# Third layer's attention: the exponential's bias and the reciprocals made for two tiles at once on VectorE

## The reference, cut to what matters

```python
# third layer, h = head, q: 256 latent rows, k: 512 rows (context and latent)
s = einsum('qd,kd->qk', q[h], k[h]) * 96 ** -0.5        # q carries an RMS norm per row
p = softmax(s, axis=-1)                                  # exp(s - max) / sum
y[h] = p @ v[h]
```

## Time and profile before

| | |
|---|---|
| three runs, median (lowest to highest) | 1456.79 us (1455.14 to 1459.68) |
| profiled execution, span from first to last instruction | 1454.6 us |
| instructions | 21621 |
| busy: PE, PEld | 1403.6 us (96%), 1172.3 us (81%) |
| busy: DVE, ACT, POOL | 848.5 us (58%), 659.0 us (45%), 840.2 us (58%) |
| mean granted TensorE clock | 0.993 |

### The profile page before, as it was taken

The page is one execution under the profiler, slowest core; times in us unless marked ns, Lnnn a source line. Parts: engine busy times, 40 slices in busy tenths (PEclk is TensorE's granted clock), DMA queues, the critical chain, the costliest instruction groups (busy, mean ns, idle before and its releaser), DMA issues.

```text
span 1454.6 us, 21621 instructions
## 1 busy us (share of the span) xinstructions
PE 1403.6 (96%) x8272; PEld 1172.3 (81%) x8272; DVE 848.5 (58%) x1638; ACT 659.0 (45%) x1070; POOL 840.2 (58%) x672
## 2 busy tenths in 40 slices
PE   5999999999999999999999999999999999999998
PEld 2978789999988888546878888888888866888887
DVE  3798667776676689688675333321126768554522
ACT  3555665455453133684342232232226386544442
POOL 1533427998864444675444554544446530699997
PEclk9999999999999999999999999999999999999999
DMA  9748516777775652010445555533333320365664
GB/s 365 288 164 309 195 50 212 248 258 241 243 259 194 202 192 80 31 44 15 174 174 182 195 202 185 193 122 96 102 107 102 110 94 16 118 200 188 187 187 135
DMA packets 71207, 242.01 MB, mean 166 GB/s; under 512 B 7488, under 2 KB 12992, under 8 KB 70720
## 3 DMA queue, kind: packets, MB, share of 16 engines
q1 hardware_dynamic: 68688, 236.63, 48.1%
q10 hardware_dynamic: 2416, 4.00, 0.9%
HBM read 238.50 MB, written 1.05 MB: 165 GB/s over the span
## 4 chain that ended last, share of the span: by engine, by line
PE 52%; DVE 4%; ACT 1%; issue 0%; POOL 0%; DVEq 0%; ACTq 0%
PE bank L731 9%; PE bank L737 9%; PE bank L732 9%; PE bank L593 8%; PE bank L594 4%; PE bank L584 2%; PE bank L586 1%; PE bank L585 1%; PE bank L592 1%; PE cond_a L1124 1%; PE bank L1124 1%; DVE h_both L2239 1%; PE bank L1132 1%; PE cond_a L1185 1%; PE bank L1144 1%; PE cond_b L1144 1%
## 5 line engine op out<-in xcount | busy, mean ns | idle before, releaser
L2010 POOL TENSOR_TENSOR w_lo<-raw,w_hi 128x512 fp32r<-128x512 f32 (+2 forms) x610 | 776.8, 1302 | 581.1 <-ACT w_hi L1466 572.9
L1466 ACT ACTIVATE w_hi<-raw 128x1024 fp32r<-128x1024 f32 (+3 forms) x300 | 307.9, 1029 | 582.7 <-PE bank L737 375.2
L731 PE MATMUL bank<-h_both,w_hi 128*128 128x512 f32 (+1 forms) x1000 | 323.1, 340 | 1.2 <-ACT w_hi L1466 1.2
L732 PE MATMUL bank<-h_both,w_hi 128*128 128x512 f32 (+1 forms) x1000 | 322.5, 340 | 0.0
L731 PEld LDWEIGHTS bank<-h_both,w_hi 128*128 128x128 f32 x1000 | 188.3, 188 | 22.9 <-ACT w_hi L1466 1.4
L732 PEld LDWEIGHTS bank<-h_both,w_hi 128*128 128x128 f32 x1000 | 188.3, 188 | 21.3
L737 PE MATMUL bank<-h_both,w_lo 128*128 128x512 f32 (+1 forms) x1000 | 198.1, 340 | 0.0
L737 PEld LDWEIGHTS bank<-h_both,w_lo 128*128 128x128 f32 x1000 | 160.4, 188 | 21.4 <-POOL w_lo L2010 0.2
L2124 DVE CUSTOM_DVE_ANT_0 ada_junk<-ada_w,cond_a 128x1024 bf16<-128x1024 f32 x128 | 153.5, 1215 | 15.1 <-DVE work L2687 8.1
L2106 DVE TENSOR_TENSOR hidden_both<-work,hidden_both 128x256 fp32r<-128x256 f32 (+1 forms) x66 | 58.5, 886 | 135.0 <-ACT hidden_both L1547 135.0
L593 PE MATMUL bank<-h_both,w_hi 128*128 128x512 f32 x345 | 122.8, 394 | 0.0
(11 more groups left out here) (487 smaller groups left out, 2544.1 us busy)
## 6 DMA issues: line engine op xcount, KB each, us to landing
raw<-in_up SPq DMA_DIRECT2D x132, 512.0 KB, 3.6
ada_w<-in_ada SPq DMA_DIRECT2D x128, 512.0 KB, 4.5
raw<-in_down SPq DMA_DIRECT2D x48, 448.0 KB, 3.5
raw<-in_out SPq DMA_DIRECT2D x24, 512.0 KB, 3.5
raw<-in_down SPq DMA_DIRECT2D x24, 512.0 KB, 3.6
raw<-in_in SPq DMA_DIRECT2D x24, 512.0 KB, 3.5
arena<-in_ada SPq DMA_DIRECT2D x16, 512.0 KB, 11.8
raw<-in_uq SPq DMA_DIRECT2D x12, 384.0 KB, 3.1
```

The costliest lines, as they stand in the source:

```text
L731: pe.matmul(out, w_h[:, k - k0], hi[:, k, cols], start=(k == 0), stop=False)
L732: pe.matmul(out, w_h[:, k - k0], lo[:, k, cols], start=False, stop=False)
L1466: act.activation(part_slot(w_hi, f, u), raw_slot(f, u), ACT.Copy).then_inc(s["rounded"], 1)
L2010: pool.tensor_tensor(part_slot(w_lo, f, u)[:, a:b], raw_slot(f, u)[:, a:b], part_slot(w_hi, f, u)[:, a:b].bitcast(F32), ALU.subtract).then ...
```

## The change

Peaks and divide take two tiles (`a` even, and `a + 1`). `peaks(a)` now makes both `reduce_max`, waiting for each tile's scores before its own, and then one `tensor_scalar` on two columns that counts `att_m` up by two. `divide(a)` waits for the exponential of `a + 1`, makes one reciprocal of two columns, and then scales both tiles, each counting `att_p` up by one as before. The branch for an attention with sinks, which the third layer doesn't take, goes away. PE's and ACT's instructions and their order stay as they are.

```diff
--- before.py
+++ after.py
@@ -2555,34 +2555,24 @@
 
             swap16 = list(range(16, 32)) + list(range(16))
 
-            def attention(m, a0, heads, scale, sinks, tile0):
-                if sinks:
-                    then(dve.tensor_scalar(m["nsink"], S("sink"), -1.0, None, ALU.mult))
+            def attention(m, a0, heads, tile0):
 
                 def peaks(a):
-                    h, t = head_of(a)
-                    dve.wait_ge(s["att_s"], a0 + a + 1)
-                    if sinks:
-                        if a >= 3:
-                            dve.wait_ge(s["att_e"], a0 + a - 2)
-                        then(dve.tensor_tensor_reduce(m["masked"][a % 3], score_bank(a)[:, :],
-                                                      C0("window", 2)[:, t, :], 1.0, -3e38, ALU.add, ALU.max,
-                                                      m["peak"][:, a:a + 1]))
-                        dve.tensor_scalar(m["nmax"][:, a:a + 1], m["peak"][:, a:a + 1], -scale,
-                                          m["nsink"][:, h:h + 1], ALU.mult, ALU.min).then_inc(s["att_m"], 1)
-                    else:
-                        then(dve.reduce_max(m["peak"][:, a:a + 1], score_bank(a)[:, :], AX_X))
-                        dve.tensor_scalar(m["nmax"][:, a:a + 1], m["peak"][:, a:a + 1], m["q_minus"][:, t:t + 1], None,
-                                          ALU.mult).then_inc(s["att_m"], 1)
+                    t = head_of(a)[1]
+                    for n in (a, a + 1):
+                        dve.wait_ge(s["att_s"], a0 + n + 1)
+                        last = dve.reduce_max(m["peak"][:, n:n + 1], score_bank(n)[:, :], AX_X)
+                    then(last)
+                    dve.tensor_scalar(m["nmax"][:, a:a + 2], m["peak"][:, a:a + 2], m["q_minus"][:, t:t + 1], None,
+                                      ALU.mult).then_inc(s["att_m"], 2)
 
                 def divide(a):
-                    dve.wait_ge(s["att_e"], a0 + a + 1)
-                    one = m["total"][:, a:a + 1]
-                    if sinks:
-                        then(dve.tensor_tensor(one, one, m["esink"][:, a:a + 1], ALU.add))
-                    then(dve.reciprocal(one, one))
-                    dve.tensor_scalar(m["prob"][a % 4], m["prob"][a % 4], one, None, ALU.mult)\
-                       .then_inc(s["att_p"], 1)
+                    dve.wait_ge(s["att_e"], a0 + a + 2)
+                    two = m["total"][:, a:a + 2]
+                    then(dve.reciprocal(two, two))
+                    for n in (a, a + 1):
+                        dve.tensor_scalar(m["prob"][n % 4], m["prob"][n % 4], m["total"][:, n:n + 1], None, ALU.mult)\
+                           .then_inc(s["att_p"], 1)
 
                 def outputs(t):
 
@@ -2592,16 +2582,13 @@
                     then(copy(hi, y))
                     low(h_lo[:, tile0 + t, late], y, hi).then_inc(s["att_y"], 1)
 
-                for a in range(4):
-                    peaks(a)
+                peaks(0)
+                peaks(2)
                 divide(0)
-                divide(1)
                 for a in range(2, 2 * heads, 2):
                     divide(a)
-                    divide(a + 1)
-                    for n in (a + 2, a + 3):
-                        if n < 2 * heads:
-                            peaks(n)
+                    if a + 2 < 2 * heads:
+                        peaks(a + 2)
                     if a >= 8 and a % 4 == 0:
                         outputs(a // 4 - 2)
                 outputs(heads // 2 - 2)
@@ -3048,7 +3035,7 @@
                     last = dve.tensor_tensor(qh[LN:LQ, q::4, :], rope_q[a:b, :, :], swapped[a:b, :, :], ALU.subtract)
                 last.then_inc(s["rope_out"], 1)
                 dve.wait_ge(s["lq_scale"], 1)
-                attention(att2, 2 * AH, LH, LQ ** -0.5, False, 0)
+                attention(att2, 2 * AH, LH, 0)
 
             dve.wait_ge(s["small_in"], 16)
             dve.wait_ge(s["x_in"], 32)
```

## The result

| | before | changed |
|---|---|---|
| median (lowest to highest) | 1455.97 us (1451.4 to 1459.68, 4 runs) | 1468.9 us (1464.44 to 1473.9, 4 runs) |
| ratio, 95% interval | | 1.0082 (1.0061 to 1.0102) |
| span of the profiled execution | 1454.6 us | 1466.5 us |
| busy DVE, instructions of DVE | 848.5 us, 1638 | 848.5 us, 1606 |
| first reduction to last turned tile | 56.49 us | 69.70 us |

The account below looks back on a forecast made before the run. PE was taken as the bound at 3.61 us a pair; the new loop through DVE and ACT, 4.32, overtakes it and adds 10.8 us: 1456.8 + 10.8 = 1467.6 us, range 1463.5 to 1473.5.

Parts of the forecast that it names:

- PE's rhythm and the margin of 0.29 us: Third layer's attention: PE takes 3.61 us a pair, the loop through DVE and ACT 3.32, hidden with 0.29 to spare.
- The bias, +0.60: The first tile's bias in each pair waits for both reductions, so the loop through DVE and ACT gains 0.60 us.
- the sum: Forecast for the attention: new loop 4.32 us a pair, last turn at 1242.6 against 1231.79, +10.8 us.
- The reciprocal, +0.40: The first tile is scaled only after the second's exponential; the loop gains one scaling, 0.40 us.
- The widths, no difference: Two-column bias and reciprocal on DVE take no longer than one-column ones; bounds -0.06 to +0.18 us.
- and so do ACT's copies and its one rounding: In the attention, ACT's copies and its one rounding fit under DVE's 2.6 us.
- Start and end: Attention's first reduction at 1175.30, third reciprocal at 1185.3; last reciprocal at 1241.5, last turn at 1242.6.
- Nothing given back behind it: Behind the attention everything shifts with it; none of the 10.8 us is recovered.
- Rival 2, the clock: In the attention, PE's new idles bring its granted clock to half: up to +5.6 us, 1473.2 us; chance 12%.
- Rival 1, the count: DVE's instructions hold the loop: a pair 0.45 us shorter, showing in three pairs only, 1455.4 us; chance 5%.

## Why the prediction was right

The time lies in the range and 1.3 us from the forecast. By its steps:

- **PE's rhythm and the margin of 0.29 us**: right. 0.40 more made the loop 3.71, 0.60 more 3.91, both 4.31, and the excess over 3.61 came out as time.
- **The bias, +0.60**: right in sum, by two errors that cancel. From the first reduction to the bias it is 1.39 us and not 1.32. And the second exponential starts 0.77 behind the first, not 0.85: in the kernel before, the second exponential waits for the second bias, which comes 0.85 behind the first; the prediction had put that bias beside the exponentials and kept the 0.85. With both biases there at once ACT needs only its own 0.77. That the two errors cancel (+0.07 and -0.08) is luck. The loop was 4.31 where the sum had 4.32.
- **The reciprocal, +0.40**: right (0.79 for both scalings, 0.80 in the sum).
- **The widths, no difference**: nearly right 14 times of 16; the two-column bias is 0.23 long for 0.21, and begins 0.08 later behind its reductions than the one-column pair (1.39 against 1.31). The first took 0.35, and one took 1.11: the bound of +0.18 was too low for it by far. Both ran beside a low part of POOL's. The prediction had looked at POOL behind the attention alone.
- **"and so do ACT's copies and its one rounding"**: wrong for PE. On ACT the rounding does fit, but the copy queued behind it is what PE's turn waits for, 1.99 us, and the clock fell behind that. The rounding also lets POOL make its low part in the attention, and so brought the long bias.
- **Start and end**: from the first reduction to the third reciprocal 10.0 us in the sum, 10.3 measured (0.12 of it the long first bias); without rounding the attention is 67.6 us, and the sum has 1242.6 - 1175.3 = 67.3.
- **Nothing given back behind it**: right within the scatter of 2 us.
- **Rival 2, the clock**: it happened once and not in every period, for 1.2 us and not 5.6, and from a wait that it hadn't named. The row at the attention's first wait, on which its low chance rested, was not safe ground: the same kernel's second profile fell there. As to the Trainium skill, TensorE: Matmul & The Clock Gate, Part 4, by which the turns count less as activity: no run here separates the turns from the idle time.
- **Rival 1, the count**: out. With fewer instructions of DVE's no run was faster, three were slower by more than their intervals, and with the old number and the new order the loss stayed. The Trainium skill's advice in VectorE: DVE Perf Modes, Rules for kernel authors, to minimise the operations, doesn't decide here: 4.3 us less of DVE's work gave 0.0 us in the order where it was free of charge.

So the 13.2 us between the first two profiles are 10.8 by the sum, 0.3 more at the start, 0.9 for the long bias and 1.2 for the clock. The 0.3 and the 0.9 are in the changed kernel's second profile too, the 1.2 for the clock isn't. The measured 0.82%, 12 us, is 1.2 over the sum, as much as those two; its interval (8.9 to 14.9 us) is too wide to show that.

## What to carry to other kernels

Before two small instructions are merged, write down the loop that runs through them, start to start, with and without, and set it against the bound engine's rhythm: a merged instruction waits for the last of its inputs and holds back the first of its outputs, and what counts is the margin, here 0.29 us against 1.00. If pairs are wanted, the producer has to be moved ahead by as much (the scores and peaks of a pair earlier brought all of it back). And an engine's queue must be read for what stands behind an odd instruction: one rounding of a microsecond cost 0.9 us on VectorE, through GpSimd, and on TensorE 0.8 us of idle and a fall of the clock, which cost 1.2 us in one of two profiles.

## What the runs showed of the hardware

- A VectorE `tensor_scalar` on 128 x 2 elements from SBUF to SBUF took 1.11 or 1.12 us in four profiles, where it started some 0.15 us behind the start of a GpSimd `tensor_tensor` of 1.26 us and ended within 0.03 us of its end. It took 0.28 to 0.35 us in five other places where it started shortly before the end of one (1174.17 in the changed kernel's first profile, 1202.14 in that with the bias alone paired), again ending with it, and 0.23 us otherwise. Two on 128 x 1 elements in the same situation took 0.34 us together, as elsewhere. The Trainium skill, SBUF — State Buffer, SBUF: two separate sides, says that the pair of ports that the two engines share is locked for a whole instruction by whichever starts first, and the other blocks, if VectorE's instruction is of a kind that takes the pair; the traces agree, with 0.88 us lost, or 0.07 where GpSimd's instruction was nearly over. Why one column escapes, no run here shows.
- In these profiles the granted clock in the attention fell to 0.50 behind idles of PE of 1.66, 1.71, 1.81, 1.88, 1.99 and 2.00 us, and stayed at 1.00 behind 1.66 (twice), 1.79, 1.84, 1.89 and 1.91 us and behind all shorter ones. The length of the idle alone doesn't tell.
